# Two transformer layers on one core: when a modulation sum, the pooled products and the gates' Sigmoids are done

## The reference

```
mod = silu(c) @ w_ada + b_ada                # three parts: shift, scale, gate
h = rms_norm(x, norm_g) * (1 + scale) + shift
... y_a, y_b, y_c, y_d from h @ w_in ...
for i, (y, z) in enumerate(branches):
    yi = y * silu(z)
    merged += sigmoid(h @ w_merge[i]) * (yi @ w_br[i])
x = x + gate * (merged @ w_out)
```

```
y_conf = silu(layer_norm(conv31(a * sigmoid(b)))) @ w_pw
y_att  = forgetting_attention(q, k, v, f)
y_sc   = sc_b * conv3(sc_c * sc_h)
y_pool = (windowed mean - v) @ w_pool * pool_scale
mix = concatenate([y_conf, y_att, y_sc, y_pool]) @ w_out
```

## Time and profile before

| | us |
|---|---|
| median of 3 runs | 2808.57 |
| the 3 runs | 2806.27 to 2814.43 |
| profiled execution, time | 2809.46 |
| profiled execution, span | 2807.4 |
| TensorE matmuls, busy | 2608.7 (93%) |
| VectorE, busy | 893.2 (32%) |
| ScalarE, busy | 818.1 (29%) |
| GpSimd, busy | 871.2 (31%) |

### The profile page before, as it was taken

How to read it: one execution, slowest core, us unless ns; L and a number is a source line. 1 busy time by engine, 2 the same in 40 slices (tenths; PEclk the granted TensorE clock), 3 DMA queues, 4 the chain that set the end, 5 groups by cost and what they waited for, 6 DMA issues and landing times.

```text
span 2807.4 us, 30549 instructions
## 1 busy us (share of the span) xinstructions
PE 2608.7 (93%) x12788; PEld 2027.6 (72%) x12788; DVE 893.2 (32%) x1192; ACT 818.1 (29%) x1265; POOL 871.2 (31%) x476
## 2 busy tenths in 40 slices
PE   7798999999998888899999998898999999999896
PEld 5676778666687555587777666687888888888785
DVE  5213320333302454411127755404022222222423
ACT  4113541344322444422232432223211111111321
POOL 2122212443322212144642211245333333333633
PEclk8899999999998999999989999999999999999898
DMA  7101101000011000011212000210111111111111
GB/s 292 34 23 44 38 28 51 29 19 19 16 46 55 18 18 18 9 47 43 99 37 105 23 23 19 91 55 23 46 53 53 46 45 50 49 53 46 51 38 69
DMA packets 34439, 134.84 MB, mean 48 GB/s; under 512 B 3648, under 2 KB 4096, under 8 KB 32896
## 3 DMA queue, kind: packets, MB, share of 16 engines
q1 hardware_dynamic: 33984, 131.85, 13.7%
q10 hardware_dynamic: 320, 1.05, 0.1%
HBM read 123.45 MB, written 8.39 MB: 47 GB/s over the span
## 4 chain that ended last, share of the span: by engine, by line
PE 87%; DVE 6%; issue 3%; ACT 3%; POOL 1%; DMA 0%; POOLq 0%; SPq 0%; ACTq 0%; DVEq 0%
PE slot L706 57%; PE slot L752 12%; PE ps L913 2%; PE ps L937 2%; PE ps L898 2%; PE ps L784 2%; PE ps L976 1%; PE ps L967 1%; PE ps L980 1%; PE ps L993 1%; DVE cacc L2159 1%; PE ps L923 1%; PE ps L827 1%; PE ps L810 1%; POOL wlo L1554 1%
## 5 line engine op out<-in xcount | busy, mean ns | idle before, releaser
L706 PE MATMUL slot<-xhi,whi 128*128 128x512 f32 x2192 | 718.6, 410 | 50.8 <-DVE xlo L2226 15.3
L1554 POOL TENSOR_TENSOR wlo<-raw,whi 128x1024 fp32r<-128x1024 f32 (+1 forms) x169 | 432.9, 2562 | 904.3 <-ACT whi L1183 904.3
L706 PE MATMUL slot<-xlo,whi 128*128 128x512 f32 x2192 | 693.5, 398 | 0.0
L706 PE MATMUL slot<-xhi,wlo 128*128 128x512 f32 x2192 | 689.0, 396 | 0.0
L706 PEld LDWEIGHTS slot<-xhi,whi 128*128 128x128 f32 x2192 | 406.0, 193 | 151.7 <-issue 70.0
L706 PEld LDWEIGHTS slot<-xlo,whi 128*128 128x128 f32 x2192 | 422.6, 193 | 92.8
L706 PEld LDWEIGHTS slot<-xhi,wlo 128*128 128x128 f32 x2192 | 421.0, 192 | 92.2
L1183 ACT ACTIVATE whi<-raw 128x1024 fp32r<-128x1024 f32 (+1 forms) x169 | 186.3, 1103 | 353.5 <-PE slot L752 173.9
L1360 ACT ACTIVATE ptr<-ps 128x256 f32<-128x256 f32 (+3 forms) x176 | 79.9, 454 | 276.3 <-PE ps L913 275.9
L752 PE MATMUL slot<-uhi,whi 128*128 128x512 f32 x512 | 158.4, 390 | 0.0
L752 PE MATMUL slot<-ulo,whi 128*128 128x512 f32 x512 | 157.8, 389 | 0.0
(11 more groups left out here) (325 smaller groups left out, 2879.9 us busy)
## 6 DMA issues: line engine op xcount, KB each, us to landing
raw<-wstream SPq DMA_DIRECT2D x129, 512.0 KB, 3.3
raw<-wstream SPq DMA_DIRECT2D x40, 640.0 KB, 3.8
ada<-wada SPq DMA_DIRECT2D x7, 1024.0 KB, 19.9
mm<-xT SPq DMA_DIRECT2D x2, 2048.0 KB, 9.7
ada<-wada SPq DMA_DIRECT2D x2, 2048.0 KB, 27.2
mm<-xT SPq DMA_DIRECT2D x8, 512.0 KB, 4.7
res_dram<-mm SPq DMA_DIRECT2D x8, 512.0 KB, 3.0
res<-res_dram SPq DMA_DIRECT2D x8, 512.0 KB, 7.3
```

Of the source, the lines that this page charges most:

```text
L706: o = mm_(outs[:, half * HALF:(half + 1) * HALF], w[b % 2][:, k_w, :], x[:, k_x, half * HALF:(half + 1) * HALF], start=first and j == 0, s ...
L1554: tt(flat(wlo[b % 2])[:, 0:n], (raw1 if b == 1 else raw)[:, 0:n], flat(whi[b % 2])[:, 0:n].bitcast(F32), ALU.subtract).then_inc(w_lo, 1)
```

## The change

It has three parts. The third modulation sum is cut in two: VectorE's products stay where they were (`gate_mod`), TensorE's sum and the bias (`gate_sum`) come behind part 0 of Bv0. ScalarE's Sigmoid of the merge blocks of D, B, C and A is queued behind part 7, and no longer behind part 9. The pooled products become two steps `poolpw` of weight 1.0 between `conf` 2 and `conf` 3, in `ps6` and `ps7`; VectorE evicts them in halves; the order of the positions in `mix` is now pooled (6, 7), attention (2, 3), short convolution (4, 5), conv (0, 1), and ScalarE waits for each source by itself.

```
     if ev[0] == "stick" and ev[1] < NSTICK:
         return 1.0 + (HALF - stick_q0(ev[1])) / P
-    return {"pause": 2.5, "row": 0.7, "fprep": 1.0}.get(ev[0], 2.0)
+    return {"pause": 2.5, "row": 0.7, "fprep": 1.0, "poolpw": 1.0}.get(ev[0], 2.0)
...
-    tl += spread(proj_events("B"), ret)
+    proj = proj_events("B")
+    tl += proj[:1] + [("gate_sum",)] + spread(proj[1:], ret)
...
-    tl += spread(dense_part_events(["Esc1", "Esb1"])[:-2], [("conf", n) for n in range(5)])
+    closing = [("conf", 0), ("conf", 1), ("conf", 2), ("poolpw", 0), ("poolpw", 1), ("conf", 3), ("conf", 4)]
+    tl += spread(dense_part_events(["Esc1", "Esb1"])[:-2], closing)
...
-        mix_sources = [(4, scy[:, 0, :]), (5, scy[:, 1, :]), (0, cu[:, 0, :]), (1, cu[:, 1, :]),
-                       (2, yfm[:, 0, :]), (3, yfm[:, 1, :]), (6, sx[:]), (7, su[:])]
+        mix_sources = [(6, sx[:]), (7, su[:]), (2, yfm[:, 0, :]), (3, yfm[:, 1, :]),
+                       (4, scy[:, 0, :]), (5, scy[:, 1, :]), (0, cu[:, 0, :]), (1, cu[:, 1, :])]
+        mix_steps = {6: 1, 7: 2, 0: 3, 1: 4}
...
-                elif ev[0] == "gate_mod":
+                elif ev[0] == "gate_sum":
                     pe.wait_ge(mod_done, 1)
                     modulation(2).then_inc(mod_mm, 1)
...
-                elif ev[0] == "mix":
-
-                    pe.wait_ge(s_norm, NPAIR)
-                    pe.wait_ge(m_pw_in, 2)
-                    for t in range(2):
-                        pe.wait_ge(pl_done, t + 1)
-                        if t:
-                            pe.wait_ge(m_pool_in, 1)
-                        for half in range(2):
-                            o = mm_(psb[half], wpls[:, t, :], (sx, su)[t][:, half * HALF:(half + 1) * HALF],
-                                    start=True, stop=True)
-                        o.then_inc(m_pool, 1)
+                elif ev[0] == "poolpw":
+
+                    t = ev[1]
+                    pe.wait_ge(pl_done, t + 1)
+                    pe.wait_ge(pw_in, 32)
+                    if t:
+                        pe.wait_ge(m_pool_in, 2)
+                    for half, bank in enumerate((ps6, ps7)):
+                        o = mm_(bank[:], wpls[:, t, :], (sx, su)[t][:, half * HALF:(half + 1) * HALF],
+                                start=True, stop=True)
+                    o.then_inc(m_pool, 1)
...
-                    if last_part(ev):
+                    merged = BLOCKS[ev[1]][0] == "M" and BLOCKS[ev[1]][1][0] != "g"
+                    if ev[2] == 7 if merged else last_part(ev):
                         evacuate(ev[1])
...
-                    act.wait_ge(sc_done, 2)
                     for pos, (k, src) in enumerate(mix_sources):
-                        if 2 <= pos < 4 or pos >= 6:
-                            act.wait_ge(mix_src, pos - 1 if pos < 4 else pos - 3)
-                        elif pos >= 4:
+                        if k in (4, 5):
+                            act.wait_ge(sc_done, k - 3)
+                        elif k in (2, 3):
                             act.wait_ge(s_norm, NPAIR)
+                        else:
+                            act.wait_ge(mix_src, mix_steps[k])
                         split_wide(k, src)
...
+                elif ev[0] == "gate_sum":
                     dve.wait_ge(mod_mm, 2)
...
-                    split_wide(3, 0, 4, scy[:, 0, :])
-                    split_wide(3, 2, 0, cu[:, 0, :])
-                    split_wide(3, 4, 2, yfm[:, 0, :])
-                    for t in range(2):
-                        dve.wait_ge(m_pool, t + 1)
-                        v.tensor_scalar((sx, su)[t][:], ps4[:], v_("pool_scale", t, 1), None, ALU.mult
-                                        ).then_inc(m_pool_in, 1)
-                        dve.wait_ge(m_pool_in, t + 1)
-                        v.tensor_copy(token[:, 0:1], token[:, 1:2]).then_inc(mix_src, 1)
-                    split_wide(3, 6, 6, sx[:])
+                    for pos in range(0, NC, 2):
+                        split_wide(3, pos, *mix_sources[pos])
+                elif ev[0] == "poolpw":
+                    t = ev[1]
+                    dve.wait_ge(m_pool, t + 1)
+                    for half, bank in enumerate((ps6, ps7)):
+                        v.tensor_scalar((sx, su)[t][:, half * HALF:(half + 1) * HALF], bank[:], v_("pool_scale", t, 1),
+                                        None, ALU.mult).then_inc(m_pool_in, 1)
+                    dve.wait_ge(m_pool_in, 2 * t + 2)
+                    v.tensor_copy(token[:, 0:1], token[:, 1:2]).then_inc(mix_src, 1)
```

## The result

| | before | after |
|---|---|---|
| median of 4 runs, us | 2810.89 | 2782.99 |
| the 4 runs | 2806.27 to 2814.43 | 2781.08 to 2784.48 |
| profiled execution: time, span | 2809.46, 2807.4 | 2781.08, 2779.3 |

The account below looks back on a forecast made before the run. TensorE, busy 93% of the span, was taken as the bound, so only its waits and the half clock after them pay. Terms -10.0 - 7.2 - 5.5 + 2.6 + 2.3 = -17.8 us gave 2791 us, range 2782 to 2803.

Parts of the forecast that it names:

- 1, the sum: Third modulation sum: nine parts cover 12.3 of 15.5 us, a POOL split slows VectorE; -10.0 us, bounds -12.3 and -7.5.
- 2, branch B and Cm0: Earlier Sigmoids end TensorE's waits after Bm0, Bm6 and Cm0: -1.5, -5.7 and -5.5 us.
- 2, Cm2 to Cm7: Branch C's later merge blocks: the Sigmoid now stands before softmax pieces and delays copies; +2.6 us, bounds -1 and +9.
- 3, the pooled products: Between conf 2 and conf 3: waits of 5.0 us at product 1, 4.5 at x0; +2.3 us, bounds -6 and +5.
- (a): Rival: pooled products find VectorE free, so their part is -6 instead of +2.3; 2783 us, chance 0.12.
- (b): Rival: Bm0, Bm6 and Cm0 wait for something else, 12.7 us less gain; 2803.5 us, chance 0.09.
- (c): Rival: moved Sigmoid with both loads, 3.6 us, lands whole on TensorE's path in B and C; 2824 us, chance 0.04.
- (d): Rival: modulation sum at its bound -12.3 us, rest as forecast; 2789 us, chance 0.75 together with the forecast.

Follow-up runs that it names:

- sum alone: Only the third modulation sum moved behind Bv0.0, against the kernel before: 2801.49 us, ratio 0.9969.
- sum and gates: The moved sum and the moved Sigmoids without the pooled products, against the kernel before: 2779.24 us, ratio 0.9897.
- loads held: Changed kernel plus a small ScalarE copy ahead of each merge gate's Sigmoid, so the table load cannot run before the wait: 2793.55 us, 0.9941 to the kernel before.
- pooled early: Changed kernel with both pooled products between conf 0 and conf 1: 2787.87 us, ratio 0.9917 to the kernel before.
- pooled apart: Changed kernel with one pooled product on either side of conf 2: 2775.37 us, ratio 0.9882 to the kernel before.
- the gates alone: Only the merge blocks' Sigmoids moved behind part 8 of 10, against the kernel before: 2794.84 us, ratio 0.9949.
- with the split held: Changed kernel with GpSimd's low split of Bq0 held until the third sum's last multiply-add: 2779.49 us, ratio 0.9890 to the kernel before.

## Why the prediction was right, and where it was off

The direction and the range held, and so did the mechanism in the sum, branch B, Cm0 and the pooled products; in Cm2 to Cm7 it did not. The forecast of 2791 was 8 us too high. By its own steps:

**1, the sum: forecast -10.0, measured -9.2.** Its parts are in the rows: 13.28 us for the products (forecast 13.3), 5.03 us of waiting (forecast 5.2). The same instructions in this stretch gave -9.2, -11.4, -10.7, -10.9 and -12.1 in the traces of five other kernels (sum alone, sum and gates, loads held, pooled early, pooled apart); the last three gave 3.5 to 5.2 us back in the blocks up to 354. In all six TensorE stands 5.6 us in the stretch (15.8 before); what differs is half clock, 13.7 to 17.1 us of it, and where it falls. So the size holds within some 3 us. What the forecast took as given, that the rest of the wait must be paid, is another thing: with three parts more ahead of the sum the wait falls by 4.3 us and the stretch by 9.0.

**2, branch B and Cm0: forecast -1.5, -5.7, -5.5, measured -1.6, -6.0, -6.0.** Right, with the half clock behind Bm6's wait counted as it should be; Cm0 gave 0.5 more than the forecast's upper bound. Timeline of the changed kernel, ScalarE before Bm7 (answers to the earlier trace rows), and the stretches around Bm7's start (answers to the earlier trace rows):

```profile
716.47 1.28 ACT L1277 ACT_TABLE_LOAD   x1
717.76 1.03 ACT L1277 ACTIVATE zs<-slot 128x1024 f32<-128x1024 f32 x1
```

```profile
720.00:727.00 7.00, 7.00 (x30) 4.77 (x30) 4.53 (x7) 3.19 (x7) 4.40 (x4) 1.00 0.00 0
727.00:734.00 7.00, 7.00 (x28) 4.41 (x27) 3.03 (x3) 2.43 (x5) 3.79 (x5) 1.00 0.24 75
```

**2, Cm2 to Cm7: forecast +2.6, measured -6.7.** This is the step that failed, with the wrong sign, and it holds most of the difference: 9.3 us of the 10.3 between -17.8 and the traces' -28.1 (to the end of Cm7 10.0), while norm2's surplus and the misses of part 3 and the start nearly cancel. I had put load and Sigmoid, 2.3 us, in front of ScalarE's copies, as they stood in a row, where both wait for one tile. In Cm4, Cm5 and Cm6 ScalarE has idle time ahead of the gate half (in the run with the small copy this waits 0.95, 3.24 and 3.14 us), and the load runs there; in Cm2 and Cm7 the copy waits for nothing and nothing is hidden. Only the Sigmoid's 1.0 us is in the way in Cm5 and Cm6, which gives TensorE waits of 0.34 us; behind that of Cm5 the clock stays at 1.00. In Cm4 it waits 0.90 us. The waits of 2.03 and 0.47 us of the earlier trace rows go. The copy that forces the load back behind its wait turns -6.7 into +3.95. The sign is sure, the size less so: in ten kernels with the moved Sigmoids and free loads the stretch was between -3.9 and -6.7, and the changed kernel's is at the upper end of it.

**Norm2: forecast 0, measured -2.9.** It is -2.8 to -3.1 in all eleven kernels with the moved Sigmoids, the one with its loads held too, and 0.0 in the two without. TensorE stands only 0.5 us less in it than before (12.5 and 13.0 us); the rest is clock. The stretch behind branch A's last block in the kernel before, then in the changed one, 28 us ahead:

```profile
1335.00:1340.00 5.00, 3.28 (x10) 2.24 (x11) 4.56 (x2) 0.93 (x1) 5.00 (x3) 0.66 0.73 224
1340.00:1345.00 5.00, 5.00 (x16) 3.96 (x15) 0.00 (x0) 0.00 (x0) 5.00 (x3) 0.66 0.91 329
...
1425.00:1430.00 5.00, 4.21 (x32) 4.05 (x30) 1.28 (x1) 3.20 (x3) 0.00 (x0) 0.87 0.31 108
```

```profile
1307.00:1312.00 5.00, 4.62 (x11) 3.13 (x11) 3.86 (x2) 0.20 (x1) 5.00 (x2) 0.50 0.79 261
1312.00:1317.00 5.00, 5.00 (x23) 4.12 (x23) 0.00 (x0) 0.00 (x0) 5.00 (x3) 1.00 0.97 348
...
1395.00:1400.00 5.00, 4.21 (x37) 4.05 (x36) 1.28 (x1) 3.20 (x3) 0.00 (x0) 1.00 0.33 108
```

The waits there are nearly the same (2.54, 2.54 and 1.49 us in the one, 2.54, 3.11 and 0.38 in the other), but half clock is over earlier, when the matmuls come thick: 23 in five us, not 16. That it comes with the moved Sigmoids is shown, since the gates alone have it; by what path they shift half clock is open.

**3, the pooled products: forecast +2.3, measured +3.7.** Right in each place: 5.18 us of waiting at product 1 (forecast 5.0), 4.83 at x0 (4.5). Most of the difference is half clock behind x0's wait: 90.10 - 87.08 = 3.0 us, where I had taken 1.9. TensorE stands as long in this stretch as before (12.8 and 12.9 us): the whole loss is that it now stands twice, with half clock behind each.

**The rivals.** (a) The pooled products found VectorE busy, as the forecast said, so the 2783 that (a) names was hit by chance: it came about in another way. (b) and (c) are out: the gains at Bm0, Bm6 and Cm0 came, and the waits of TensorE behind a moved Sigmoid in branch C are 0.3 to 0.9 us, not (c)'s 3.6. (d), the sum at -12.3, needs that GpSimd leaves VectorE alone: with the split held the stretch is -13.1.

The Trainium skill (ScalarE: Activation LUTs, section "What ACT_TABLE_LOAD costs") was cited for 2.66 us a switch. Here the Sigmoid starts 1.29 us after the load's start when nothing else is awaited (716.47 and 717.76), and in Cm5, where the load runs ahead of the wait, it costs nothing on the path. The measurement decides.

## What to carry to other kernels

Price a function that needs a table load by where its wait for data falls: here the load ran ahead of that wait in idle time, so that only the function itself delayed what was behind it. Before moving work "into idle time" of an engine, look at what its queue holds at that moment: here 4.6 us of convolution decided on either side of which step a 1.4 us eviction could stand. And price a long wait on TensorE with the matmuls at half clock behind it. The 2.47 us before Bm7 were worth 6.0 us with their clock, and the 4.3 us at the sum 9.0; the 0.34 us of Cm5 cost no clock at all.

## What was not expected of the hardware

The table load starts before the wait of its function is met (1062.80 and 1066.02), and making the wait come first costs some 11 us over the kernel. And the place of half clock can shift in a stretch whose instructions are the same: +2.1 us in the sum's stretch in a kernel that changes nothing in it, -3.9 to -6.7 between Cm2 and Cm6, -2.9 at norm2. A sum of single terms can't be surer than that.
